# Attention with a third head in flight, and a norm without its split

## The reference, cut to what matters

```python
def _modulate(x, shift, scale):
    return _rmsnorm(x) * (1 + scale[:, None, :]) + shift[:, None, :]

# neighbourhood attention, one row of the grid
s = einsum(q_r, k_g) + bias
p = softmax(s)
o = einsum(p, v_g)

# latent attention
down = h @ w_down                 # 1024 -> 256 + 128 + 32
c_q, c_kv, k_rope = ...
s = (q_nope @ k_nope + q_rope @ k_rope) * scale
p = softmax(s); o = p @ v
```

## Time and profile before

| | |
|---|---|
| median of 3 runs | 1869.54 us (1869.36 to 1870.1) |
| the profiled execution, its own time | 1870.19 us |
| its span | 1868.4 us |
| PE busy | 1669.5 us (89%) |
| DVE busy | 1272.5 us (68%) |
| ACT busy | 869.9 us (47%) |
| POOL busy | 167.9 us (9%) |
| mean granted TensorE clock | 0.941 |

### The profile page before, as it was taken

The page is one execution under the profiler, slowest core; times in us unless marked ns, Lnnn a source line. Parts: engine busy times, 40 slices in busy tenths (PEclk is TensorE's granted clock), DMA queues, the critical chain, the costliest instruction groups (busy, mean ns, idle before and its releaser), DMA issues.

```text
span 1868.4 us, 26397 instructions
## 1 busy us (share of the span) xinstructions
PE 1669.5 (89%) x10960; PEld 1476.0 (79%) x10960; DVE 1272.5 (68%) x1531; ACT 869.9 (47%) x1008; POOL 167.9 (9%) x187
## 2 busy tenths in 40 slices
PE   7999996718699998988899996877999999999997
PEld 6999995517589997964799994345999999999996
DVE  5777745975567777533577763235788887987986
ACT  5334434221143335333533342234777777767765
POOL 1000001523000000024000001252000000000000
PEclk9999997958799999978999997989899999999998
DMA  8777550010058784520387751002698999889983
GB/s 318 283 256 277 190 184 17 1 68 1 14 232 321 277 302 166 181 91 0 148 329 253 280 213 56 1 1 87 247 360 311 333 334 332 330 333 328 340 323 140
DMA packets 51786, 385.70 MB, mean 206 GB/s; under 512 B 5873, under 2 KB 6209, under 8 KB 7761
## 3 DMA queue, kind: packets, MB, share of 16 engines
q1 hardware_dynamic: 50400, 376.16, 54.9%
q0 software_dynamic: 1264, 7.82, 1.1%
HBM read 382.90 MB, written 1.05 MB: 205 GB/s over the span
## 4 chain that ended last, share of the span: by engine, by line
PE 74%; DVE 13%; ACT 6%; issue 3%; POOL 2%; DMA 1%; DVEq 0%; ACTq 0%; SPq 0%; POOLq 0%
PE bank L296 20%; PE bank L298 19%; PE bank L297 19%; PE bank L1149 4%; PE bank L455 2%; DVE sb_wlo L268 1%; ACT sb_whi L264 1%; PE bank L1662 1%; PE bank L1623 1%; DVE sb_wlo L2090 1%; DVE sb_xn L1130 1%; PE bank L1775 1%; PE bank L1834 1%; POOL sb_h L1644 1%; PE bank L609 1%
## 5 line engine op out<-in xcount | busy, mean ns | idle before, releaser
L268 DVE TENSOR_TENSOR sb_wlo<-sb_raw,sb_whi 128x2048 fp32r<-128x2048 f32 x137 | 313.9, 2292 | 201.7 <-ACT sb_whi L264 201.7
L296 PE MATMUL bank<-sb_xhi,sb_whi 128*128 128x256 f32 x1392 | 395.7, 284 | 7.3 <-DVE sb_wlo L268 6.9
L297 PE MATMUL bank<-sb_xlo,sb_whi 128*128 128x256 f32 x1392 | 394.6, 283 | 0.0
L298 PE MATMUL bank<-sb_xhi,sb_wlo 128*128 128x256 f32 x1392 | 394.5, 283 | 0.0
L264 ACT ACTIVATE sb_whi<-sb_raw 128x2048 fp32r<-128x2048 f32 x137 | 261.7, 1910 | 199.6 <-PE bank L298 193.8
L296 PEld LDWEIGHTS bank<-sb_xhi,sb_whi 128*128 128x128 f32 x1392 | 267.8, 192 | 9.8 <-DVE sb_wlo L268 7.7
L297 PEld LDWEIGHTS bank<-sb_xlo,sb_whi 128*128 128x128 f32 x1392 | 267.9, 192 | 1.1
L298 PEld LDWEIGHTS bank<-sb_xhi,sb_wlo 128*128 128x128 f32 x1392 | 267.8, 192 | 0.0
L296 PE MATMUL bank<-sb_whi,sb_slots_hi 128*128 128x256 f32 x896 | 257.8, 288 | 0.0
L298 PE MATMUL bank<-sb_whi,sb_slots_lo 128*128 128x256 f32 x896 | 252.7, 282 | 0.0
L297 PE MATMUL bank<-sb_wlo,sb_slots_hi 128*128 128x256 f32 x896 | 251.7, 281 | 0.0
(11 more groups left out here) (474 smaller groups left out, 2662.8 us busy)
## 6 DMA issues: line engine op xcount, KB each, us to landing
sb_raw<-in_ffn SPq DMA_DIRECT2D x98, 1024.0 KB, 5.3
sb_raw<-in_moe SPq DMA_DIRECT2D x86, 1024.0 KB, 5.5
sb_ada_raw<-in_ada SPq DMA_DIRECT2D x32, 1536.0 KB, 6.9
sb_cst<-in_moe SPq DMA_DIRECT2D x28, 1024.0 KB, 5.3
sb_xn<-in_moe SPq DMA_DIRECT2D x27, 1024.0 KB, 5.1
sb_ada_raw<-in_moe SPq DMA_DIRECT2D x27, 1024.0 KB, 5.2
sb_raw<-in_w_in SPq DMA_DIRECT2D x13, 1024.0 KB, 4.9
sb_raw<-in_na_qk SPq DMA_DIRECT2D x8, 1024.0 KB, 4.9
```

The lines of the kernel that those rows point to most:

```text
L268: e.tensor_tensor(wlo[s][:, :], raw[s][:, :], whi[s][:, :], ALU.subtract).then_inc(s_lo[s], 1)
L296: e.matmul(dst, wh, xh, start=first, stop=False, skip_group_check=skip)
L297: e.matmul(dst, wh, xl, start=False, stop=False, skip_group_check=skip)
L298: return e.matmul(dst, wl, xh, start=False, stop=last, skip_group_check=skip)
```

## The change

The steps of the attention loop are staggered over four iterations in place of three. The inverse of the sums and POOL's multiplications become a step of their own, `normalised`, one iteration behind the scores; the transposes stand two and the values three iterations behind. The loop has one iteration more. Then the norm ahead of the latent attention takes the form "alone", whose marks now have semaphores of their own; the down product takes the tiles of `xn` in the order in which they come, each with its own mark, and writes banks 4 to 6, since banks 0 to 3 still hold what ACT and DVE read.

```diff
         def spread(added, gain, shift, keep, act_at=(), dve_at=()):
-            d0, t0, x0 = tally["diag"] - NB, tally["turned"], tally["xn"]
+            d0, t0, x0, h0 = tally["diag"] - NB, tally["turned"], tally["xn"], tally["alone"]
             tally["turned"] += KT // 2
-            tally["xn"] += KT
+            tally["alone" if keep == "alone" else "xn"] += KT // 2 if keep == "alone" else KT
...
-                        e.activation(xn[:, k, :], tile(k), ACT.Identity, scale=gain(k), bias=shift(k)).then_inc(s_xn, 1)
+                        e.activation(xn[:, k, :], tile(k), ACT.Identity, scale=gain(k), bias=shift(k)).then_inc(s_half_act, 1)
...
-                        e.tensor_scalar(xn[:, k, :], tile(k), gain(k), shift(k), ALU.mult, ALU.add).then_inc(s_low, 1)
+                        e.tensor_scalar(xn[:, k, :], tile(k), gain(k), shift(k), ALU.mult, ALU.add).then_inc(s_half_dve, 1)
...
-                return [((s_xn, s_low)[k % 4 // 2], x0 + 2 * (k % 2) + k // 4 + 1) for k in range(KT)]
+                return [((s_half_act, s_half_dve)[k % 4 // 2], h0 + 2 * (k % 2) + k // 4 + 1) for k in range(KT)]
...
-        m = norm(acc, "row", M(1, 1), M(1, 0), True, row=flat_xn[:, 0:D], m_row=(s_kept, 1))
+        m = norm(acc, "row", M(1, 1), M(1, 0), "alone", row=flat_xn[:, 0:D], m_row=(s_kept, 1))
         acc, m_row, m_row2 = latent(env, m)
...
         for q in range(NB):
-            m2 = act.step(lambda e, q=q: e.activation(sb_[:, q, :], src[:, q, :], ACT.Exp, bias=mx[:, i, q:q + 1],
-                                                      scale=scale, accum_out=mx[:, i, 2 + q:3 + q]),
-                          m1, m_tr.get(i - 3))
+            m_exp[i] = act.step(lambda e, q=q: e.activation(sb_[:, q, :], src[:, q, :], ACT.Exp, bias=mx[:, i, q:q + 1],
+                                                            scale=scale, accum_out=mx[:, i, 2 + q:3 + q]),
+                                m1, m_tr.get(i - 3))
         if bias is None:
-            m_sread[i] = m2
-        m3 = dve.step(lambda e: e.reciprocal(mx[:, i, 2:4], mx[:, i, 2:4]), m2)
+            m_sread[i] = m_exp[i]
+
+    def normalised(i):
+        m3 = dve.step(lambda e: e.reciprocal(mx[:, i, 2:4], mx[:, i, 2:4]), m_exp[i])
         for q in range(NB):
-            m3 = pool.step(lambda e, q=q: e.tensor_scalar(sb_[:, q, :], sb_[:, q, :], mx[:, i, 2 + q:3 + q], None,
-                                                          ALU.mult), m3)
+            m3 = pool.step(lambda e, q=q: e.tensor_scalar(s[i % 3][:, q, :], s[i % 3][:, q, :], mx[:, i, 2 + q:3 + q],
+                                                          None, ALU.mult), m3)
         m_nrm[i] = m3
...
-    for i in range(AH + 2):
+    for i in range(AH + 3):
         if i < AH:
             softmax(i)
         if 0 <= i - 1 < AH:
-            transposed(i - 1)
+            normalised(i - 1)
         if 0 <= i - 2 < AH:
-            weigh(i - 2)
+            transposed(i - 2)
+        if 0 <= i - 3 < AH:
+            weigh(i - 3)
         follow(i)
...
-            outs = [(bank[0][:, 0:T], 0, P), (bank[0][:, T:2 * T], P, P), (bank[1][:, 0:T], 2 * P, P),
-                    (bank[2][0:ROPE, 0:T], 3 * P, ROPE)]
+            outs = [(bank[4][:, 0:T], 0, P), (bank[4][:, T:2 * T], P, P), (bank[5][:, 0:T], 2 * P, P),
+                    (bank[6][0:ROPE, 0:T], 3 * P, ROPE)]
             for o, at, n in outs:
-                for k_ in range(KT):
-                    m = pe.step(lambda e, o=o, at=at, n=n, k_=k_: e.matmul(
-                        o, wd[:, k_, at:at + n], y[:, k_, :], start=k_ == 0, stop=k_ == KT - 1), gd, m_in[-1])
+                for n_, k_ in enumerate((0, 4, 2, 6, 1, 5, 3, 7)):
+                    m = pe.step(lambda e, o=o, at=at, n=n, k_=k_, n_=n_: e.matmul(
+                        o, wd[:, k_, at:at + n], y[:, k_, :], start=n_ == 0, stop=n_ == KT - 1), gd, m_in[k_])
```

More of the change, by code:

```diff
@@ L336, in build_program @@
         s_dummy = sem("root_table")
-        tally = {"acc": 0, "sum": 0, "scaled": 0, "stat": 0, "diag": 0, "turned": 0, "xn": 0, "table": 0}
+        s_half_act, s_half_dve = sem("xn_by_act"), sem("xn_by_dve")
+        tally = {"acc": 0, "sum": 0, "scaled": 0, "stat": 0, "diag": 0, "turned": 0, "xn": 0, "table": 0, "alone": 0}
         HALVES = [(b, f) for b in range(NB) for f in range(2)]
@@ L1770, in latent @@
                    dma(pool, wuq, a["mla_uq"], "uq", (env["s_ada"], ADA_UNITS), m_in[-1])]
-            outs = [(bank[0][:, 0:T], 0, P), (bank[0][:, T:2 * T], P, P), (bank[1][:, 0:T], 2 * P, P),
-                    (bank[2][0:ROPE, 0:T], 3 * P, ROPE)]
+            outs = [(bank[4][:, 0:T], 0, P), (bank[4][:, T:2 * T], P, P), (bank[5][:, 0:T], 2 * P, P),
+                    (bank[6][0:ROPE, 0:T], 3 * P, ROPE)]
             for o, at, n in outs:
-                for k_ in range(KT):
-                    m = pe.step(lambda e, o=o, at=at, n=n, k_=k_: e.matmul(
-                        o, wd[:, k_, at:at + n], y[:, k_, :], start=k_ == 0, stop=k_ == KT - 1), gd, m_in[-1])
-            m1 = act.step(lambda e: e.activation(lat[:, 0:2, :], bank[0][:, :].rearrange("p (k t) -> p k t", k=2),
+                for n_, k_ in enumerate((0, 4, 2, 6, 1, 5, 3, 7)):
+                    m = pe.step(lambda e, o=o, at=at, n=n, k_=k_, n_=n_: e.matmul(
+                        o, wd[:, k_, at:at + n], y[:, k_, :], start=n_ == 0, stop=n_ == KT - 1), gd, m_in[k_])
+            m1 = act.step(lambda e: e.activation(lat[:, 0:2, :], bank[4][:, :].rearrange("p (k t) -> p k t", k=2),
                                                  ACT.Copy), m)
-            m2 = act.step(lambda e: e.activation(lat[:, 2, :], bank[1][:, 0:T], ACT.Copy), m)
-            m3 = dve.step(lambda e: e.tensor_copy(kr[0:ROPE, :], bank[2][0:ROPE, 0:T]), m)
+            m2 = act.step(lambda e: e.activation(lat[:, 2, :], bank[5][:, 0:T], ACT.Copy), m)
+            m3 = dve.step(lambda e: e.tensor_copy(kr[0:ROPE, :], bank[6][0:ROPE, 0:T]), m)
             meet()
```

## The result

The changed kernel takes 1827.03 us, median of four runs (1826.18 to 1828.75), beside 1869.45 us for the kernel before (1867.53 to 1870.1, four runs). The ratio is 0.9776, with an interval of 0.9759 to 0.9793.

A forecast was written before the change was run, and what follows sets the result against it. No engine bounded the loops; the latency of one head with two in flight did, 3.50 us a head in the second. Gains of 10.8 + 16.2 + 6.9 = 33.9 us led from 1869.54 to 1835.6, said as 1836; range 1828 to 1850.

The forecast's parts named there:

- the mechanism and its cycle: Attention loops: scores over the previous head's late inverse, POOL and transposes to scores sets the pace, 3.07 and 2.96 us a head.
- the norm: Norm ahead of the latent attention: 4.6 us of pause and 2.3 us of half clock go, 6.9 us together.
- The pause: Between the last turning matmul and the down product: PE's 4.62 us wait for DVE's split of eight tiles goes.
- the sum: Whole kernel: gains of 10.8 (second loop), 16.2 (first loop) and 6.9 us (norm), 33.9 together, leading to 1835.6 us.
- the low clock at the start of both loops: Loop starts: 16.2 us at 1.2 GHz in the first, 6.6 lost; 5 us in the second, 2.5 lost.
- The first loop: First attention loop, first to last transposes: 46.4 us plus 6.6 lost to low clock, 53.0 against 69.19, a 16.2 us gain.
- less low clock than now: Rival: both loop starts have short low clock and the norm gains in full, 1829 us; 12%.
- PE alone 2.86 us, so PE is 97% busy: Second loop: PE's own work is 1.26 us of scores plus 1.60 of transposes and values, just under the 2.96 pace.
- The clock keeps falling: Rival: denser loops keep their low-clock shares, losing another 5.5 and about 2 us: 1843, up to 1850 us; 25%.
- The third head does not help: Rival: what stands behind the maxima keeps the loops' pace at 3.5 us a head, 1855 us; 4%.
- Slower by the clock: Rival: PE's clock stays low throughout both loops, PE bounds at 5.18 us a head in the first, 1890 us; 3%.
- Nothing given back: After the loops: DMA is idle in them and the next loads move up with PE, so no gain is lost.

The follow-up runs named there:

- inverse-at-once kernel: Changed kernel with the inverse and POOL's multiplication moved back into the iteration of their own scores, three heads still in flight: 1835.46 us.
- kernel with the norm alone: Changed kernel with the old attention loop, so only the new norm and down product against the kernel before: 1862.84 us.
- loops-alone kernel: Kernel before with the new attention loop, norm and down product left as they were: 1834.33 us.
- the unused matmuls: Changed kernel plus matmuls with unused results in PE's idle time ahead of the first transposes, six in the first loop, two in the second: 1825.56 us.
- the gaps filled: Kernel before plus matmuls with unused results at both loop starts and ahead of every second head's transposes, order of heads unchanged: 1855.94 us.
- copy-first kernel: Changed kernel with inverse and multiplication in their own scores' iteration, behind the copy of head i - 2, gate product ahead of the multiplication: 1825.17 us.
- inverse behind the maxima with two heads: Changed kernel without the third head, inverse still one iteration behind the scores, transposes in that same iteration, values in the next: 1974.02 us.
- warm start: Kernel before plus ten matmuls with unused results in PE's idle time ahead of the first loop's first transposes: 1868.09 us.
- best kernel: The copy-first kernel plus matmuls with unused results ahead of the first transposes, six in the first loop, two in the second: 1818.57 us.

## Why the prediction was right, and where it was wrong

**Right: the mechanism and its cycle.** The pace of the loops is the new cycle from the scores over the late inverse of the head before to its transposes: 2.905 and 3.01 us a head, 2.96 and 3.07 forecast. The difference is mostly that I let the inverse start 0.17 us behind the scaling, and it starts 0.08 behind (1217.87 to 1217.95). The inverse-at-once kernel shows the cycle by taking the late inverse out of it: the transposes cease to wait. The gate product came first on POOL and its sum lay in the idle start.

**Right: the norm.** 7.1 us measured alone, 6.9 forecast. The down product lost exactly the 2.3 us of half clock. The pause gave 4.6 in the sum; measured it is 5.8 in the changed kernel, since there the turning ran partly at the full clock as well (5.39 us in place of 6.37), and 4.9 in the kernel with the norm alone, where it took 6.28. That is no merit of the shorter loops: with them it took 5.22 us in the loops-alone kernel and 6.26 with the inverse at once.

**The step that failed: the low clock at the start of both loops.** In "The first loop" I took 16.2 us at 1.2 GHz again, 6.6 of them lost. It was 6.2 us, and 2.7 lost, as the unused matmuls show. In the second loop I took 5 us, 2.5 lost. The first transposes took 0.66 us and the clock was 1.00 from the first to the last, so nothing was lost. Together 6.4 of the 7.7 us by which the loops beat the sum.

For the second loop the rows show a likely reason. In the kernel before, the clock had risen in the microsecond at 1216 and fell again at 1219 (0.75), in the idle 4.35 us ahead of the first transposes. In the changed kernel the gate sum and the third scores fill that time: the clock is low from 1183 to 1187, back at 0.98 in the microsecond at 1187, and only 1.11 us of idle time follow before the transposes at 1189.80. I had moved this work into the idle start in the sum, and had left the clock there as it was.

For the first loop I had read the 16 us as a property of the start that any order would meet again. The runs show that the length goes with the order, 13.0 and 16.3 us with the old one and 6.0 to 6.3 with the new. Why is not shown. The later low stretches of the kernel before, from 850.9, 861.1 and 878.2, came behind waits of 1.50 to 1.66 us, and with the gaps filled there was none. The change leaves waits of 0.39 and 0.58 us in the middle of the loops, and there was none either. The rival "less low clock than now" had the outcome right, priced at 6.6 us below the forecast; I gave it 12% and the range stopped 1 us short of the result. That the median lies so near the rival's 1829 is in part luck: the stretches outside the loops move by more than that.

The Trainium skill (TensorE: Matmul & The Clock Gate, A second HAM failure mode: psum-queue depth-cycling) tells of a kernel whose frequent short idle times between groups of matmuls make the clock go up and down, and of the cost of that. The trace agrees here: the loops with gaps ran at 0.78 and 0.92, the same loops with filled gaps at 1.00. The rule of the Trainium skill (the same page, Part 1: The HAM clock gate) that activity releases the low clock, which I had held up against the sum, pointed the right way for the new loops. It does not explain the 16 us of a PE without a gap at half clock.

**Smaller terms.** First loop at the full clock: 46.4 forecast, 45.94 measured. Second: 44.9 against 43.93. In the second, from the scores of head 3 to those of head 15 it was 1227.60 - 1190.29 = 37.3 us in place of 38.8, 0.7 of the difference from the pace and 0.8 from the gate sums, which come to about 0.8 each where I had 1.1. From the last scores to their transposes it was 6.13 in place of 5.40, since POOL does head 14's multiplication first. "PE alone 2.86 us, so PE is 97% busy" was wrong for the second loop: PE alone is 2.50. The 1.26 us of the scores held a wait that PE's row does not name. The row of the weight load behind them does; POOL's multiplication for that head ended at 1264.90:

```profile
1264.95 0.42 PEld L1652 LDWEIGHTS bank<-sb_cst,sb_s_mla 128*128 128x128 f32 x4 [0.54 <-POOL sb_s_mla L1644]
```

(In the first loop the 2.79 was right: 2.78 in the copy-first kernel.) PE is busy in 38.80 of 43.93 us, 88%. It cost nothing, since the cycle decides either way, but it hid the 4.7 us that a better order still finds.

**The other rivals.** "The clock keeps falling", my second likeliest at 25%, is out: both loops are at 0.94 and 1.00. "The third head does not help" is out by 11.6 and 10.8 us at equal clock. "Slower by the clock" did not come for this kernel. The inverse behind the maxima with two heads shows that it is a real danger of this loop: clock 0.59 and 0.69, and 103 us more than the kernel before.

**Nothing given back** holds within what can be told. Stretches outside the loops differ by up to 5 us between kernels, whatever the edit: from the last transposes to the end it was 589.2 us in the norm-alone kernel, 589.4 before, 593.2 with the loops alone, 589.7 with the unused matmuls, and 594.5 in the kernel before with its gaps filled. Runs of one and the same kernel differ as much: the loops-alone kernel from 1833.85 to 1838.4 us, the inverse-at-once kernel from 1827.61 to 1836.22. I did not find what sets them. That stays open, and so does why the clock stays down for 13 to 16 us under a busy PE in the old order and for 6 in the new.

## What to carry to other kernels

When a loop on PE waits for another engine every few microseconds, price the wait twice: once by its length, and once by the granted clock of the whole loop beside the same work at the full clock. Here the second price was 11.6 of 20.5 us in one loop, and filling all its gaps with unused matmuls shows it in one run, or even pays by itself. Filling the start alone gave next to nothing in the kernel before. And when a latency is hidden by one more item in flight, look at what is queued behind what on each helper engine: the order maxima, copy, inverse, with the gate product ahead of the multiplication, gave 4.7 us more in the second loop than the one that was made, from the same operations.

## What the runs showed of the hardware that was not expected

- A PE whose rows show no gap can stay at 1.2 GHz for long: 16.3 us from 820.9 to 837.2 in the kernel before, 13.0 us in the norm-alone kernel, and nearly 14 of the 16 us from 829 to 845 (clock 0.57, busy 16.00 of 16.00 us) with the warm start. With the new order of the same work it was 6.0 to 6.3 us.
- Gaps well under 2 us can go with a fall of the clock, but do not always. In the first loop of the kernel before it fell at or behind the waits that end at 850.79, 860.73 and 876.90 (1.66, 1.65 and 1.50 us), and not behind those that end at 842.45 and 869.61 (1.66 both). The changed kernel's waits of 0.4 to 0.6 us leave it at 1.00, and yet it fell behind waits of 0.57 and 0.53 us in the best kernel. No run separates one gap from what stands ahead of it.
- Unused matmuls in all its gaps made a kernel 14.3 us faster (1870.23 to 1855.94), with both loops at 1.00 in place of 0.78 and 0.92.
- A start-to-start time on PE can hold a wait that its row does not name: the scores that I took as 1.26 us of PE's own time took 0.97 in the loop where PE does not wait (1208.17 to 1209.14). The row of the weight load names the wait.
